# Turning the experts' gate and up results by threes instead of one wave at a time

## The chip, the cores and the metric

The kernel runs on one NeuronCore of a Trainium2 chip. The number that counts is the device time of one execution in microseconds (us); lower is better. TensorE (PE in the profile) multiplies, VectorE (DVE) and ScalarE (ACT) work element by element, GpSimd (POOL) does a few side jobs, and SyncE (SP) issues the DMA transfers. TensorE writes its results to PSUM, which has eight banks of 512 float32 numbers in each of 128 partitions; the other engines copy them from there to SBUF.

## The reference

Two layers of a decoder over 264 tokens (256 of a prompt, 8 of samples). The change lies in the last sub-layer of the second one, a mixture of eight experts of which each token uses two:

```python
def moe_swiglu(h, w_router, w_gate, w_up, w_down):
    logits = jnp.einsum('bld,de->ble', h, w_router).astype(jnp.float32)
    top_val, top_idx = lax.top_k(logits, TOP_K)          # TOP_K = 2
    gate = jax.nn.softmax(top_val, axis=-1)
    ...
    for e in range(N_EXPERTS):                           # 8
        act = jax.nn.silu(h @ w_gate[e]) * (h @ w_up[e])  # 1024 -> 1408 columns, twice
        out = out + combine[..., e:e + 1] * (act @ w_down[e])
    return out
```

Everything is float32. The token mixers, the cross-attention and the dense feed-forward of layer 0 fill the first three quarters of the time and are the same in both kernels.

## The kernel before

**Places, slots and waves.** The router's choices put each token into two of 768 places (`PLACES`). 32 places are a slot, which belongs to one expert: 8 slots are fixed, one for each expert, and 16 are free and go to experts that have more tokens than a slot holds. Four slots are a wave, so there are six waves (`WAVES`), of 128 places each.

**Pieces.** The experts' weights come in 66 pieces of 2 MB, each with a 128-row block of all eight experts' weights, 512 columns of each. 44 of them (`GU_PIECES`) are for gate and up: a column group `c_` has 256 gate and 256 up columns (`GU_COLS` = 256), and needs eight pieces, one for each 128 rows of the 1024; there are five such groups (`GU_FULL` = 5) and a last one with 128 columns of each, in four pieces. 22 pieces are for the down product. They lie in a ring of four places in the tile `big`; SP issues piece p when piece p-4 is no longer read (line 492). Since a free slot's expert is only known at run time, VectorE (11 of 16) and ScalarE (5 of 16) first copy the cells of the free slots to fixed addresses in `stream` and `nrm` (`copies`, lines 2273 and 1666), wave by wave, for waves 2 to 5 of the next piece.

**A wave on TensorE** (`wave`, line 1180) is four matmuls, one for each slot, of 32 places by 512 columns. Each uses 32 columns of the array, so the four run side by side; each is two instructions in the profile, so a wave has eight. Its results are added up over the pieces of a group in bank w of PSUM, for wave w.

**The end of a group.** After the group's last piece, ScalarE takes silu of the gate half of bank w (`silu`, line 1674), VectorE multiplies it with the up half (`multiply`, line 2282) into the tile `m_a[w]` (a part of `tmp`). The result has places on partitions, and the down product needs it with columns on partitions. So TensorE turns it (`turn`, line 1165): two transposes of 128 x 128, which use the full array (one in the last group). They go to bank 6 or 7 in turn, and ScalarE (line 1682, even waves) or VectorE (line 2290, odd waves) copies them to `acts`, in `turned_in`.

**The order** is written out by hand on each engine. TensorE does the turns of a group during the first piece after it: the wave w of that piece, which overwrites bank w, then the turn w. That is in pieces 8, 16, 24, 32, 40 and 44. A turn waits for the multiplication of its wave (`m_act`) and for the eviction of the turn two before it (`m_even`, `m_odd`), since this had the same bank. VectorE and ScalarE take each instruction in its written order: in such a piece they go through w = 0 to 5, copy for the next piece where w is 2 or more, and evict the turn of the same w.

Of the kernel before, what the change touches and what calls it, by code (L numbers as in the profile page):

```python
# [24 lines left out]
P = 128  # L25
# [49 lines left out]
WAVES = (FIXED + FREE) // 4  # L75
PLACES = (FIXED + FREE) * SLOT
GU_COLS, GU_FULL = CELL // 2, F_TILES * P // (CELL // 2)
# [9 lines left out]
def gu_piece(p):  # L87

    return (p // KT, (p % KT,)) if p < GU_FULL * KT else (GU_FULL, (2 * (p - GU_FULL * KT), 2 * (p - GU_FULL * KT) + 1))


def gu_ends(p):

    return 0 <= p < GU_PIECES and KT - 1 in gu_piece(p)[1]
# [43 lines left out]
def program(nc, t):  # L138

    with ExitStack() as ctx:  # L140
# [116 lines left out]
        m_silu, m_act, m_turn = sem("m_silu"), sem("m_act"), sem("m_turn")  # L257
        m_even, m_odd = sem("m_even"), sem("m_odd")
# [9 lines left out]
        def bank(b, lo=0, n=512, rows=P, r0=0):  # L268
            return ps[r0:r0 + rows, b * 512 + lo:b * 512 + lo + n]
# [50 lines left out]
        ident, ones = c(C_ID), c(C_ONES)  # L320
# [111 lines left out]
        m_sig, m_a = ([tmp[:, GU_COLS * k:GU_COLS * (k + 1)] for k in range(a, z)] for a, z in ((0, 2), (2, 2 + WAVES)))  # L432
# [6 lines left out]

        def turned(n, cols):  # L440

            return bank(6 + n % 2, 0, cols)

        lin_of, piece_of, n, q = {}, {}, 0, 0
        for name, k, pieces in (("in", N_PROJ, 1), ("out", KT, 2), ("memk", KT, 1), ("q", KT, 1), ("memv", KT, 1), ("o", KT, 1)):
            lin_of[name], piece_of[name] = n, q
            n, q = n + k, q + k * pieces
# [126 lines left out]
        def _(pe):  # L574
# [62 lines left out]
            for l in range(DEPTH):  # L637
# [414 lines left out]
                for mt in range(2):  # L1052
                    ins = pe.transpose(bank(7, mt * P, P), csP[:, mt * P:(mt + 1) * P], ident)
# [14 lines left out]
                for dt in range(2):  # L1068
                    ins = pe.transpose(bank(7, dt * P, P), csO[:, dt * P:(dt + 1) * P], ident)
# [40 lines left out]
                for k in range(KT):  # L1110
                    pe.wait_ge(h_full, (3 * l + 2) * KT + k + 1)
                    ins = pe.matmul(bank(7, 0, NT, NE), wrt[:, k * NE:(k + 1) * NE], tile(tmp, k), start=k == 0, stop=k == KT - 1)
# [42 lines left out]
                                            start=tt == 0, stop=tt == 2, skip_group_check=True)  # L1155
                    ins.then_inc(gx, 1)

                def turn(c_, w):

                    n, cols = WAVES * c_ + w, GU_COLS if c_ < GU_FULL else P  # L1160
                    pe.wait_ge(m_act, n + 1)
                    if n >= 2:
                        pe.wait_ge((m_even, m_odd)[w % 2], n // 2)
                    for f in range(cols // P):
                        ins = pe.transpose(turned(n, cols)[:, f * P:(f + 1) * P], m_a[w][:, f * P:(f + 1) * P], ident)  # L1165
                    ins.then_inc(m_turn, 1)

                def wave(p, w, dst, rows, first, last, parts=1):

# [23 lines left out]
                for p in range(GU_PIECES):  # L1193
                    c_, ks = gu_piece(p)
                    if p < KT - 1:
                        gather(p + 1)
                    elif p == KT - 1:
                        slot_sums()
                    if p < KT:
                        pe.wait_ge(gx_act, p + 1)  # L1200
                        pe.wait_ge(gx_dve, p + 1)
                    for w in range(WAVES):
                        if ks[0] == 0 and c_:
                            pe.wait_ge(m_act, WAVES * (c_ - 1) + w + 1)
                        wave(p, w, w, lambda part: xg(ks[part]), ks[0] == 0, ks[-1] == KT - 1, len(ks))
                        if ks[0] == 0 and c_:
                            if (c_, w) == (1, 0):
                                pe.wait_ge(slots_in, 1)
                            turn(c_ - 1, w)
                for h in range(2):  # L1210
                    for f in range(F_TILES):
                        p = GU_PIECES + h * F_TILES + f
                        for w in range(WAVES):
                            if (h, f) == (0, 0):
                                pe.wait_ge(m_act, WAVES * GU_FULL + w + 1)
                            if h == 0 and w == 0 and f * P % GU_COLS == 0:
                                pe.wait_ge(m_even, (f * P // GU_COLS + 1) * WAVES // 2)
                                pe.wait_ge(m_odd, (f * P // GU_COLS + 1) * WAVES // 2)
                            elif (h, f) == (1, 0):
                                pe.wait_ge(out_lo, w + 1)  # L1220
                            wave(p, w, w, lambda part: acts(f), f == 0, f == F_TILES - 1)
                            if (h, f) == (0, 0):
                                turn(GU_FULL, w)
                        if h == 1 and 1 <= f <= 4:
                            if f == 1:
                                pe.wait_ge(out_lo, WAVES)
                                pe.wait_ge(picks, BACK)
                            elif f >= 3:
                                pe.wait_ge(m_add, f - 2)
                            scatter(0, f - 1, 6 + (f - 1) % 2)  # L1230
                        elif h == 1 and f == 7:
                            pe.wait_ge(m_add, KT // 2)
                            for j in range(KT // 2):
                                norm_part((l + 1) * NORMS, j, tmp)
# [12 lines left out]
        def _(act):  # L1247
# [35 lines left out]
            for l in range(DEPTH):  # L1283
# [222 lines left out]
                for j in range(KT):  # L1506
                    n = L0 + lin_of["memk"] + j
# [5 lines left out]
                for j in range(KT):  # L1513
                    n = L0 + lin_of["q"] + j
# [161 lines left out]
                def turned_in(c_, w):  # L1676

                    n, cols = WAVES * c_ + w, GU_COLS if c_ < GU_FULL else P
                    act.wait_ge(m_turn, n + 1)
                    f0 = c_ * (GU_COLS // P)  # L1680
                    dst = proj[:, ACTS + f0 * PLACES:ACTS + (f0 + cols // P) * PLACES].rearrange("p (f s) -> p f s", f=cols // P)[:, :, w * P:(w + 1) * P]
                    act.activation(dst, turned(n, cols).rearrange("p (f s) -> p f s", f=cols // P), ACT.Copy).then_inc(m_even, 1)
# [8 lines left out]
                for p in range(-1, PIECES_X):  # L1691
                    if 0 <= p < KT - 1:
                        gather_in(p + 1)
                    for w in range(WAVES):
                        if gu_ends(p):
                            act.wait_ge(wave_done, WAVES * p + w + 1)
                            silu(gu_piece(p)[0], w)
                        elif p - GU_PIECES in (F_TILES - 1, DOWN_PIECES - 1):
                            act.wait_ge(wave_done, WAVES * p + w + 1)
                            out_high((p - GU_PIECES) // F_TILES, w)  # L1700
                        if w >= 2 and p + 1 < PIECES_X:
                            copies(p + 1, w)
                        if w % 2 == 0 and p > 0 and gu_ends(p - 1):
                            turned_in(gu_piece(p - 1)[0], w)
                    if p == GU_PIECES + F_TILES + 5:
                        act.preload_act_table_set("natural_log_exp_and_others")
                        for j in range(KT // 2):
                            act.wait_ge(m_add, j + 1)
                            square(j, xT, tmp)
# [7 lines left out]
        def _(dve):  # L1717
# [42 lines left out]
            for l in range(DEPTH):  # L1760
# [523 lines left out]
                def turned_in(c_, w):  # L2284

                    n, cols = WAVES * c_ + w, GU_COLS if c_ < GU_FULL else P
                    dve.wait_ge(m_turn, n + 1)
                    f0 = c_ * (GU_COLS // P)
                    dst = proj[:, ACTS + f0 * PLACES:ACTS + (f0 + cols // P) * PLACES].rearrange("p (f s) -> p f s", f=cols // P)[:, :, w * P:(w + 1) * P]
                    dve.tensor_copy(dst, turned(n, cols).rearrange("p (f s) -> p f s", f=cols // P)).then_inc(m_odd, 1)  # L2290
# [14 lines left out]
                for p in range(-1, PIECES_X):  # L2305
                    if 0 <= p < KT - 1:
                        gather_in(p + 1)
                    if p == 0:
                        weights_in()
                    elif p == KT - 1:  # L2310
                        slots_taken()
                    f = p - GU_PIECES - F_TILES
                    for w in range(WAVES):
                        if gu_ends(p):
                            multiply(gu_piece(p)[0], w)
                        elif p - GU_PIECES in (F_TILES - 1, DOWN_PIECES - 1):
                            out_low((p - GU_PIECES) // F_TILES, w)
                        if w >= 2 and p + 1 < PIECES_X:
                            copies(p + 1, w)
                        if w % 2 == 1 and p > 0 and gu_ends(p - 1):  # L2320
                            turned_in(gu_piece(p - 1)[0], w)
                    if 1 <= f <= 4:
                        add_scattered(0, f - 1, 6 + (f - 1) % 2)
                for d in range(4):
# [300 lines left out]
```

## Time and profile before

| | |
|---|---|
| median of 3 runs | 1625.02 us (1619.92 to 1628.04) |
| the profiled execution | 1625.43 us, of which 1623.6 us from first to last instruction |
| granted TensorE clock, mean | 0.98 |
| TensorE busy | 1515.6 us, 93% |
| VectorE, ScalarE busy | 1020.5 us (63%), 827.0 us (51%) |
| DMA, mean | 225 GB/s |

Times in the rows are us from the first instruction. A row of the timeline names an engine, a line of the kernel, an operation, the tiles written and read, and how many instructions are merged. The start of a TensorE row is where its first matmul starts to stream; the duration shown goes to the last one's modelled end, and overlaps with the next row. So distances between starts are what to read.

### The profile page before, as it was taken

The numbers are of one execution on the slowest core, as the hardware profiler recorded it, in microseconds if no ns is written. First come the engines' busy times: TensorE is split into PE (matmuls) and PEld (weight loads), VectorE is DVE, ScalarE is ACT, GpSimd is POOL, SyncE is SP. The second block draws the span as 40 slices with busy tenths as digits, with TensorE's granted clock in tenths as the row PEclk, the third lists the DMA queues.
The fourth block names the chain that finished last, engine by engine and source line by source line (L and its number), as shares of the span: only waits on it lengthen the run. The fifth ranks groups of instructions, "written<-read, shape, count | busy, mean of one in ns | idle before, by whom it ended". The sixth has DMA issues, their size and how long they took to land.

```text
span 1623.6 us, 31559 instructions
## 1 busy us (share of the span) xinstructions
PE 1515.6 (93%) x12739; PEld 1178.2 (73%) x12739; DVE 1020.5 (63%) x2060; ACT 827.0 (51%) x1597; POOL 308.2 (19%) x301
## 2 busy tenths in 40 slices
PE   6999987899999999999999878999879999999998
PEld 5999965799878999989999667998754322234333
DVE  4855589555245565668555886552356777777765
ACT  4445547545344454544455465453424566665654
POOL 3992224200000000039912232000000100000000
PEclk9999999999999999999999999999989999999999
DMA  8455445554774464454554355547746899999982
GB/s 322 156 182 169 147 143 178 178 206 158 295 300 149 154 203 173 157 202 156 182 172 145 143 166 188 205 159 282 306 175 215 311 378 390 384 382 360 402 341 82
DMA packets 52069, 365.14 MB, mean 225 GB/s; under 512 B 5973, under 2 KB 10645, under 8 KB 22997
## 3 DMA queue, kind: packets, MB, share of 16 engines
q1 hardware_dynamic: 49732, 355.97, 59.6%
q0 software_dynamic: 2192, 7.15, 1.3%
q8 instruction: 102, 1.67, 0.4%
q14 instruction: 43, 0.34, 0.1%
HBM read 338.62 MB, written 24.48 MB: 224 GB/s over the span
## 4 chain that ended last, share of the span: by engine, by line
PE 84%; DVE 9%; ACT 3%; DMA 2%; issue 2%; SPq 0%; DVEq 0%; ACTq 0%
PE ps L1180 21%; PE ps L606 17%; PE ps L607 16%; PE ps L608 16%; DVE stream L1964 3%; PE ps L586 2%; DVE proj L2025 1%; PE ps L1145 1%; DMA ring<-w_o_dram 1%; PE ps L1165 1%; PE ps L997 1%; PE ps L971 1%; PE ps L1188 1%; DMA ring<-w_v_dram 1%; PE ps L873 1%
## 5 line engine op out<-in xcount | busy, mean ns | idle before, releaser
L317 DVE TENSOR_TENSOR wL<-ring,wH 128x1024 fp32r<-128x1024 f32 x284 | 357.6, 1263 | 322.6 <-ACT wH L311 320.6
L606 PE MATMUL ps<-hH,wH 128*128 128x264 f32 x1376 | 401.7, 292 | 14.6 <-DVE hL L1736 7.8
L607 PE MATMUL ps<-hL,wH 128*128 128x264 f32 x1376 | 393.6, 286 | 0.0
L608 PE MATMUL ps<-hH,wL 128*128 128x264 f32 x1376 | 393.2, 286 | 0.0
L311 ACT ACTIVATE wH<-ring 128x1024 fp32r<-128x1024 f32 x284 | 298.0, 1054 | 120.1 <-PE ps L608 109.6
L606 PEld LDWEIGHTS ps<-hH,wH 128*128 128x128 f32 x1376 | 262.3, 191 | 22.9 <-issue 19.7
L607 PEld LDWEIGHTS ps<-hL,wH 128*128 128x128 f32 x1376 | 263.0, 191 | 0.6
L608 PEld LDWEIGHTS ps<-hH,wL 128*128 128x128 f32 x1376 | 261.8, 190 | 0.0
L606 PE MATMUL ps<-projR,wH 128*128 128x264 f32 (+1 forms) x816 | 239.6, 294 | 15.7 <-DVE projR L2126 7.1
L607 PE MATMUL ps<-projR,wH 128*128 128x264 f32 (+1 forms) x816 | 233.7, 286 | 0.0
L608 PE MATMUL ps<-projR,wL 128*128 128x264 f32 (+1 forms) x816 | 233.1, 286 | 0.0
L1281 ACT ACTIVATE proj<-ps 128x264 f32<-128x264 f32 (+1 forms) x160 | 62.5, 390 | 277.4 <-PE ps L608 277.4
L2273 DVE COPY stream<-big 128x512 f32 x396 | 140.9, 424 | 86.9 <-PE ps L1180 86.8
L606 PEld LDWEIGHTS ps<-projR,wH 128*128 128x128 f32 x816 | 156.6, 192 | 19.9 <-DVE projR L2126 7.6
L607 PEld LDWEIGHTS ps<-projR,wH 128*128 128x128 f32 x816 | 156.7, 192 | 0.8
L608 PEld LDWEIGHTS ps<-projR,wL 128*128 128x128 f32 x816 | 156.3, 192 | 0.0
L1666 ACT ACTIVATE stream<-big 128x512 f32 x132 | 83.1, 631 | 113.8 <-PE ps L1180 113.8
L1666 ACT ACTIVATE nrm<-big 128x512 f32 x198 | 117.5, 626 | 30.7 <-PE ps L1180 30.7
L1180 PE MATMUL ps<-nrm,proj 128*32 128x512 f32 (+1 forms) x1120 | 127.1, 569 | 0.3 <-issue 0.3
L1180 PE MATMUL ps<-big,proj 128*32 128x512 f32 (+1 forms) x1120 | 127.1, 570 | 0.0
L1180 PE MATMUL ps<-stream,proj 128*32 128x512 f32 (+1 forms) x1120 | 126.8, 569 | 0.0
L2273 DVE COPY nrm<-big 128x512 f32 x330 | 117.8, 422 | 1.4 <-PE ps L1180 1.4
(372 smaller groups left out, 1907.8 us busy)
## 6 DMA issues: line engine op xcount, KB each, us to landing
big<-x_gu_dram SPq DMA_DIRECT2D x44, 2048.0 KB, 9.6
ring<-w_in_dram SPq DMA_DIRECT2D x56, 1024.0 KB, 4.8
big<-x_down_dram SPq DMA_DIRECT2D x22, 2048.0 KB, 9.8
ring<-w_gu_dram SPq DMA_DIRECT2D x22, 1024.0 KB, 4.8
stream<-states_dram SPq DMA_DIRECT2D x32, 512.0 KB, 4.1
ring<-w_out_dram SPq DMA_DIRECT2D x16, 1024.0 KB, 4.9
o_states_dram<-stream SPq DMA_DIRECT2D x32, 512.0 KB, 3.2
ring<-kc_dram SPq DMA_DIRECT2D x16, 1024.0 KB, 6.5
```

The costliest lines, as they stand in the source:

```text
L311: act.activation(wH[:, buf * PIECE:buf * PIECE + n], slot(s, half * n, n), ACT.Copy).then_inc(hi_ready, 1)
L317: dve.tensor_tensor(wL[:, buf * PIECE:buf * PIECE + n], slot(s, half * n, n), f32(wH[:, buf * PIECE:buf * PIECE + n]), ALU.subtract).then_ ...
L586: ins = pe.matmul(bank(6, 0, w), ones, tile(src, s0 + j, 0, w), start=j == 0, stop=j == KT - 1, skip_group_check=True)
L606: pe.matmul(dst, wh, high(k0 + k), start=k0 + k == 0, stop=False)
L607: pe.matmul(dst, wh, low(k0 + k), start=False, stop=False)
L608: ins = pe.matmul(dst, wl, high(k0 + k), start=False, stop=k0 + k == k_all - 1)
L873: ins = pe.matmul(bank(7, 0, NT), ones, nrm[:, post_tile(p) + j * NT:post_tile(p) + (j + 1) * NT], start=j == 0, stop=j == tiles - 1)
L1180: ins = pe.matmul(ps[32 * q:32 * q + 32, dst * 512:dst * 512 + n], rows(part)[:, b * SLOT:(b + 1) * SLOT], src, start=first and part == 0, ...
L1281: act.activation(dst, src, func, scale=scale).then_inc(lin_free[n % 2], 1)
L1666: ins = act.activation(copy_of(j), big[:, bass.ds(source[j] + BIG_ORDER[p % 4] * BIG, CELL)], ACT.Copy)
L1964: ins = dve.scalar_tensor_tensor(out=S[:, at * P:(at + 1) * P], in0=bank(hf, b * P, P), scalar=k[:, at:at + 1], in1=S[:, at * P:(at + 1) * ...
L2273: ins = dve.tensor_copy(copy_of(j), big[:, bass.ds(source[j] + BIG_ORDER[p % 4] * BIG, CELL)])
```

## The change

Turns are now made by threes. After wave 2 of the piece come the turns of waves 0, 1 and 2, and after wave 5 those of waves 3, 4 and 5. Three turns need three places in PSUM, and six of them are cycled through banks 6 and 7: `turned` puts turns 0 to 5 in banks 6, 7, 6, 7, 6, 7, at columns 0, 0, 256, 256, 0, 0, so two turns share a bank. No engine may read a bank while a turn is written to its other half: all evictions therefore wait for the last turn of their three (`turned_with`), and the second three waits for all evictions of the first. VectorE and ScalarE evict at w = 2 and w = 5 of their loops, behind the copies for that w: ScalarE turns 0 and 2, VectorE turn 1, and then ScalarE turn 4, VectorE turns 3 and 5.

```diff
         def turned(n, cols):
-            return bank(6 + n % 2, 0, cols)
+            return bank(6 + n % 2, n % WAVES // 2 % 2 * GU_COLS, cols)
+
+        def turned_with(n):
+            return n // 3 * 3 + 3
...
-                def turn(c_, w):
-                    n, cols = WAVES * c_ + w, GU_COLS if c_ < GU_FULL else P
-                    pe.wait_ge(m_act, n + 1)
-                    if n >= 2:
-                        pe.wait_ge((m_even, m_odd)[w % 2], n // 2)
-                    for f in range(cols // P):
-                        ins = pe.transpose(turned(n, cols)[:, f * P:(f + 1) * P], m_a[w][:, f * P:(f + 1) * P], ident)
-                    ins.then_inc(m_turn, 1)
+                def turn_three(c_, w0):
+                    cols, before = GU_COLS if c_ < GU_FULL else P, WAVES // 2 * c_
+                    if w0:
+                        pe.wait_ge(m_even, before + 2)
+                        pe.wait_ge(m_odd, before + 1)
+                    elif c_:
+                        pe.wait_ge(m_even, before)
+                        pe.wait_ge(m_odd, before)
+                    for w in range(w0, w0 + 3):
+                        n = WAVES * c_ + w
+                        pe.wait_ge(m_act, n + 1)
+                        for f in range(cols // P):
+                            ins = pe.transpose(turned(n, cols)[:, f * P:(f + 1) * P], m_a[w][:, f * P:(f + 1) * P], ident)
+                        ins.then_inc(m_turn, 1)
...
                         if ks[0] == 0 and c_:
-                            if (c_, w) == (1, 0):
+                            if (c_, w) == (1, 2):
                                 pe.wait_ge(slots_in, 1)
-                            turn(c_ - 1, w)
+                            if w % 3 == 2:
+                                turn_three(c_ - 1, w - 2)
...
-                            if (h, f) == (0, 0):
-                                turn(GU_FULL, w)
+                            if (h, f) == (0, 0) and w % 3 == 2:
+                                turn_three(GU_FULL, w - 2)
...
-                    act.wait_ge(m_turn, n + 1)
+                    act.wait_ge(m_turn, turned_with(n))
...
-                        if w % 2 == 0 and p > 0 and gu_ends(p - 1):
-                            turned_in(gu_piece(p - 1)[0], w)
+                        if w % 3 == 2 and p > 0 and gu_ends(p - 1):
+                            for v in ((0, 2), (4,))[w // 3]:
+                                turned_in(gu_piece(p - 1)[0], v)
...
-                    dve.wait_ge(m_turn, n + 1)
+                    dve.wait_ge(m_turn, turned_with(n))
...
-                        if w % 2 == 1 and p > 0 and gu_ends(p - 1):
-                            turned_in(gu_piece(p - 1)[0], w)
+                        if w % 3 == 2 and p > 0 and gu_ends(p - 1):
+                            for v in ((1,), (3, 5))[w // 3]:
+                                turned_in(gu_piece(p - 1)[0], v)
```

TensorE's program in piece 16, from its wave 0 on, before (`ps<-const,tmp` 128x128 is a transpose, and the other rows are the four matmuls of a wave):

```order
L1180 MATMUL ps<-big,proj 32x512 [waits landed3,m_act]
L1180 MATMUL ps<-big,proj 32x512 x3
L1165 MATMUL ps<-const,tmp 128x128 [waits m_even,m_act]
L1165 MATMUL ps<-const,tmp 128x128
L1180 MATMUL ps<-big,proj 32x512 [waits landed3,m_act]
L1180 MATMUL ps<-big,proj 32x512 x3
L1165 MATMUL ps<-const,tmp 128x128 [waits m_odd,m_act]
L1165 MATMUL ps<-const,tmp 128x128
L1180 MATMUL ps<-stream,proj 32x512 [waits copied_act,copied_dve,m_act]
L1180 MATMUL ps<-stream,proj 32x512 x3
L1165 MATMUL ps<-const,tmp 128x128 [waits m_even,m_act]
L1165 MATMUL ps<-const,tmp 128x128
```

The same place in the changed kernel, where the wave is line 1190 and the transpose line 1175:

```order
L1190 MATMUL ps<-big,proj 32x512 [waits landed3,m_act]
L1190 MATMUL ps<-big,proj 32x512 x3
L1190 MATMUL ps<-big,proj 32x512 [waits landed3,m_act]
L1190 MATMUL ps<-big,proj 32x512 x3
L1190 MATMUL ps<-stream,proj 32x512 [waits copied_act,copied_dve,m_act]
L1190 MATMUL ps<-stream,proj 32x512 x3
L1175 MATMUL ps<-const,tmp 128x128 [waits m_act,m_odd,m_even]
L1175 MATMUL ps<-const,tmp 128x128
L1175 MATMUL ps<-const,tmp 128x128 [waits m_act]
L1175 MATMUL ps<-const,tmp 128x128
L1175 MATMUL ps<-const,tmp 128x128 [waits m_act]
L1175 MATMUL ps<-const,tmp 128x128
```

The three pairs of transposes have moved together behind the third wave, and the first of them carries the waits for evictions.

VectorE's program in piece 16, before, from the last copies for this piece's own wave 5 on (line 2273 is a copy of a free slot's cell, line 2290 an eviction of a turn):

```order
L2273 COPY nrm<-big 128x512 [waits wave_done]
L2273 COPY nrm<-big 128x512
L2290 COPY proj<-ps 128x2x128 [waits m_turn]
L2273 COPY stream<-big 128x512 [waits wave_done,landed2]
L2273 COPY stream<-big 128x512 x2
L2273 COPY stream<-big 128x512 [waits wave_done]
L2273 COPY stream<-big 128x512 x2
L2290 COPY proj<-ps 128x2x128 [waits m_turn]
```

The same place in the changed kernel (copies are line 2285, evictions line 2302):

```order
L2285 COPY nrm<-big 128x512 [waits wave_done]
L2285 COPY nrm<-big 128x512
L2285 COPY stream<-big 128x512 [waits wave_done,landed2]
L2285 COPY stream<-big 128x512 x2
L2302 COPY proj<-ps 128x2x128 [waits m_turn]
L2285 COPY stream<-big 128x512 [waits wave_done]
L2285 COPY stream<-big 128x512 x2
```

The eviction of turn 1 now stands behind the first three copies for the next piece; those of turns 3 and 5 stand together behind its last two.

## Rows read from the trace of the kernel before

**Rows 1.** The chain that ended last, from 1220 us on, by line.
```profile
by line: PE ps L1180 85.9%; PE ps L1145 4.2%; PE ps L1165 3.1%; PE ps L1188 2.9%; PE ps L586 1.0%; DVE tmp L1729 0.7%; PE ps L1154 0.5%; ACT proj L1656 0.1%; issue 0.1%; ACT rstd L1267 0.1%; DVE xT L2302 0.1%; ACT rstd L1268 0.1%; ACT tmp L
```

**Rows 2.** Busy time of each engine in two stretches, granted clock, DMA share.
```profile
core 0: us, PE busy (x) PEld busy (x) DVE busy (x) ACT busy (x) POOL busy (x), PEclk, DMA share, GB/s
1225.50:1613.60 388.10, 387.84 (x3609) 135.62 (x3608) 283.77 (x814) 227.41 (x406) 6.89 (x6) 1.00 0.87 337
1333.80:1370.80 37.00, 37.00 (x346) 11.03 (x345) 27.27 (x80) 23.14 (x42) 0.00 (x0) 1.00 0.97 383
```

**Rows 3.** The instructions of line 1165, the turns, in the whole run.
```profile
L1165 PEld LDWEIGHTS ps<-const,tmp x66: 137/140/143, 1282.3 to 1489.3; 128*128 128x128 f32 x66
```

**Rows 4.** Timeline of TensorE, piece 15 and, from 1325.58, piece 16.
```profile
1320.43 1.90 PE L1180 MATMUL ps<-big,proj 128*32 128x512 f32 x16
...
1325.58 1.04 PE L1180 MATMUL ps<-big,proj 128*32 128x512 f32 x8
1326.56 0.44 PE L1165 MATMUL ps<-const,tmp 128*128 128x128 f32 x2
1326.92 1.07 PE L1180 MATMUL ps<-big,proj 128*32 128x512 f32 x8
...
1333.38 0.44 PE L1165 MATMUL ps<-const,tmp 128*128 128x128 f32 x2
```

**Rows 5.** Timeline of TensorE in piece 44: first and last of six turns.
```profile
1483.02 0.33 PE L1165 MATMUL ps<-const,tmp 128*128 128x128 f32 x1
...
1489.30 0.33 PE L1165 MATMUL ps<-const,tmp 128*128 128x128 f32 x1
```

**Rows 6.** Timeline of TensorE in the attention of the same layer.
```profile
1155.43 0.66 PE L1023 MATMUL ps<-const,conv 128*128 128x128 f32 x4
1155.93 0.60 PE L1029 MATMUL ps<-const,proj 128*128 128x128 f32 x4
1156.46 1.07 PE L987 MATMUL ps<-ring,tmp 128*32 128x256 f32 x16
```

**Rows 7.** Timelines of TensorE's matmuls and loads: 16 transposes of the router.
```profile
1204.41 1.97 PE L1119 MATMUL ps<-const,tmp 128*128 128x128 f32 x16
```
```profile
1204.41 1.73 PEld L1119 LDWEIGHTS ps<-const,tmp 128*128 128x128 f32 x16
```

**Rows 8.** Timeline of VectorE in piece 16.
```profile
1327.69 0.42 DVE L2282 TENSOR_TENSOR tmp<-tmp,ps 128x256 f32<-128x256 f32 x1
1328.02 0.76 DVE L2273 COPY nrm<-big 128x512 f32 x2
1328.69 0.42 DVE L2290 COPY proj<-ps 128x256 f32<-128x256 f32 x1
1329.49 1.10 DVE L2273 COPY stream<-big 128x512 f32 x3 [0.37 <-PE ps L1180]
```

**Rows 9.** Timeline of ScalarE in piece 16.
```profile
1329.48 0.63 ACT L1666 ACTIVATE stream<-big 128x512 f32 x1 [1.95 <-PE ps L1180]
1330.02 0.37 ACT L1682 ACTIVATE proj<-ps 128x256 f32<-128x256 f32 x1
```

**Rows 10.** Timelines of TensorE and VectorE in piece 8.
```profile
1281.35 1.04 PE L1180 MATMUL ps<-big,proj 128*32 128x512 f32 x8
```
```profile
1284.69 0.75 DVE L2273 COPY nrm<-big 128x512 f32 x2
```

**Rows 11.** DMA issues of pieces: all 54 from 1284 us on, then two alone.
```profile
DMA to landing us min/median/max: 7.9/9.9/11.0
```
```profile
L492 SPq DMA_DIRECT2D big<-x_gu_dram x1: 327/327/327, 1296.6 to 1296.6; - x1
...
DMA to landing us min/median/max: 10.4/10.4/10.4
```
```profile
L492 SPq DMA_DIRECT2D big<-x_gu_dram x1: 328/328/328, 1322.4 to 1322.4; - x1
...
DMA to landing us min/median/max: 9.5/9.5/9.5
```

## The prediction

> **What bounds the kernel now.** I read the chain of waits first, because it says which engine's faster work would move the end. From the first expert piece on it stays on TensorE: the waves have 85.9% of it and the turns (line 1165) 3.1% [rows 1]. Then the busy times over that whole stage, 1225.5 to 1613.6 us: TensorE is busy for 387.84 of 388.10 us at full granted clock (1.00, which is 2.4 GHz), VectorE for 283.77 and ScalarE for 227.41 [rows 2]. So here every microsecond taken from TensorE's stream is one off the end, unless something it waits for comes too late. One number warns: DMA is 97% busy where waves run without turns [rows 2]. I come back to it.
>
> **What a turn costs now.** Piece 15 has six waves and no turn: from 1320.43 to 1325.58 they take 0.858 us each [rows 4]. With a turn of two transposes behind each, the distance from turn to turn is (1333.38 - 1326.56) / 5 = 1.364 us [rows 4], so the turn costs 0.506. In piece 44, with one transpose, it is (1489.30 - 1483.02) / 5 = 1.256 us [rows 5], so 0.398. The difference of the two, 0.108 us, is one transpose. What is left, 0.506 - 2 x 0.108 = 0.290 us, is paid for each visit, however many transposes it has: TensorE goes from matmuls on 32 columns of the array, four side by side, to one on all 128, and back. It shows as both an entry and an exit: the turn's start is 0.98 us behind the wave's (0.12 more than 0.858), and the next wave starts 0.36 after the turn (0.15 more than two transposes) [rows 4].
>
> **What the change removes.** Six visits in each of pieces 8, 16, 24, 32, 40 and 44 are 36; now there are two in each, 12. The 66 transposes [rows 3] stay. So the sum is 24 visits x 0.290 = **7.0 us less**. It rests on two assumptions. First, that transposes in a row keep 0.108 us each. Sixteen of the router's take 1.97 us with the last one's drain of about 0.27, so (1.97 - 0.27) / 15 = 0.113, and their loads (1.73 - 0.14) / 15 = 0.106 [rows 7]; by the dearer one the 42 transposes that now follow another across a wave's or a pair's border cost at most 0.2 us more. Second, that a visit costs the same when it is longer. The trace has the very case: eight transposes between two runs of 32-column matmuls take 1156.46 - 1155.43 = 1.03 us, which is 8 x 0.108 + 0.16, one entry, although the second four belong to another line with waits of its own [rows 6]. So waits that are already satisfied, in the middle of such a run, cost nothing that I can see; I take zero, and as the dear end 0.07 us (half of a load's 0.14 [rows 3]) for each of the 24 middle waits, 1.7 us.
>
> Against this stands a rule that gives another price. It would be that a transpose cannot load while another streams, since both need all rows of the array. Then each costs its load and its stream, 0.140 [rows 3] + 0.107 (a wave streams 512 columns in two passes in 0.858 us, so 128 in one pass take 0.107) = 0.247, a pair 0.494 of the 0.506, and a visit only 0.012: the change would gain 24 x 0.012 = 0.3 us. The rows speak against it: a second transpose adds 0.108, not 0.247 [rows 4, 5], and the router's sixteen would take 3.9 us instead of 1.97 [rows 7]. By this rule the trace disagrees: the Trainium skill, page "TensorE: Matmul & The Clock Gate", section "The mechanism", says that a weight load overlaps with matmuls in flight only when its row group differs.
>
> **What the change moves, in piece 16.** TensorE first. Wave 0 starts at 1325.58 [rows 4]; three waves and the entry give 1325.58 + 2.57 + 0.12 = 1328.27 for the first three turns, six transposes and the exit 0.65 + 0.15, so wave 3 starts at 1329.07. Three more waves and an entry: the second three turns at 1331.76 us.
> - *Results needed earlier.* Wave 5 overwrites bank 5 and would start at 1330.8 instead of 1332.4. Its multiplication, the last, ends at 1328.11, and the copies for it at 1328.78 [rows 8]. Slack 2.0 us.
> - *Evictions.* The second three waits for turns 0 and 2 on ScalarE and turn 1 on VectorE. VectorE is free at 1328.78, takes the three copies for the next piece (wave 2 is done by then), 1.0 us net, and evicts in 0.42 [rows 8]: about 1330.2, 1.5 us before 1331.76. ScalarE has one copy of 0.63 and two evictions of 0.37 [rows 9], which wait for the three turns (done with drain at about 1329.2): 1330.0. Behind them on both engines wait the copies for wave 3 of the next piece, which wave 3 of this piece allows only from 1330.0 on and which are needed five microseconds later. The evictions of turns 3, 4 and 5 end at about 1333.7; nobody waits for them before the next group.
> - *Piece 8* is the tightest, since VectorE comes late out of the slot sums. Wave 0 starts at 1281.35 [rows 10], so the second three at 1287.53. VectorE is free at 1285.44 [rows 10]; copies and eviction end at about 1287.1 even at the slower copies of that place. Slack 0.4 us, once; I take no wait.
> - *DMA.* A piece is issued behind wave 1 of the piece four before, and needed by the copies three pieces and a wave later, 16 us at least; the slowest landing took 11.0 us [rows 11]. That leaves 5 us.
>
> So the sum is made against the profiled execution: 1625.43 - 7.0 = 1618.4 us. That run lies 0.4 us over the median of 1625.02, which would give 1618.0. I say **1618.2 us**, 0.43% less. The three runs of before spread over 8.1 us, which is as much as 0.5% of the time, and 0.5% is about what a measurement of this kernel can tell from no change.
>
> **The rivals.**
> 1. *Half of it.* Waits inside the threes cost their dear end (1.7 us), and in some pieces the second three waits for VectorE's eviction of turn 1, which is now in order behind three copies. It would take about 0.3 us on each of six second visits to lose another 1.8. For it: the order of VectorE, and the 0.4 us of piece 8. Against: 1.5 us of slack in the four middle ones. Time 1625.4 - 3.5 = 1621.9. Chance 0.10.
> 2. *No gain, because weights come no faster.* DMA is at 97% [rows 2], and a group's eight pieces now take 8 x 5.15 + 3.04 = 44.2 us; with the change 43.1. If 5.53 us for a piece were what the transfers can do, TensorE would wait for all that it saves: 1625.4. Against it: the six pieces issued from 1296.6 to 1322.4 us, 5.16 us apart, needed 10.4 us at first and 9.5 at the end [rows 11]. A queue that was overfed would show a rising time; so one piece takes no more than 5.16. Chance 0.05. The rule on loads above has the same result, 1625.1, with chance 0.02.
> 3. *Slower.* The evictions of the first three come so late that TensorE stands before the second three. There are six such places, so 7.0 / 6 = 1.2 us each eat the gain, and with the slack of 1.5 us that means evictions 2.7 us later than worked out above; to be 8.1 us slower it takes 2.5 us of standing, 4 us later. That could be if VectorE's copies for the next piece wait for a late landing, as these stand ahead of the eviction now: TensorE would wait for the weights of the next piece already in this one. A landing 4 us late beyond its 5 us slack has no row that speaks for it. Time, with 2.5 us each, 1633. Chance 0.03.
> 4. *More than worked out*, as when fewer switches also free a few tenths in the waves between: 1616. Chance 0.02.
>
> **How the numbers follow.** The forecast has 0.78. Its own range is 1614 to 1622, the sum's bounds (a gain of 5.1, with both dear ends, to 7.2 us, with the rounding of the starts) and some 3 us for medians of few runs. The range for 8 in 10 goes further on both sides for the runs' own spread and takes in rival 1: 1612 to 1624.5. The bound for faster by over 0.5% lies at 1616.9, only 1.3 us from the forecast, so about four in ten of its chance and rival 4 fall there: 0.32. Slower by over 0.5% is rival 3 and a bad draw: 0.04. The rest is 0.64.
>
> **What the profile after would show.** Line 1175 with 66 transposes in runs of six (three in piece 44), each run and its exit about 0.80 us from its start to that of the next wave. From wave 0 of piece 16 to wave 0 of piece 17 about 7.0 us instead of 8.2. TensorE's loads idle before line 1175 twelve times instead of 36. VectorE's and ScalarE's evictions each behind their three, and no wait of TensorE for `proj` over 0.1 us. Landings still 8 to 11 us. The forecast is wrong if transposes inside a run are further apart than 0.12 us, if line 1175 waits for `proj` (VectorE or ScalarE), or if waves wait for the ring's DMA.

## The result, and the profile after

| | before | changed |
|---|---|---|
| median | 1624.19 us (1616.90 to 1629.89, 16 runs) | 1616.35 us (1610.48 to 1621.95, 16 runs) |
| profiled execution, span | 1623.6 us | 1618.7 us |

The ratio is 0.9954, with a 95% interval from 0.9938 to 0.9970: 7.5 us less, with 4.9 to 10.1 in the interval. The sum said 7.0. The kernel before was run again beside the experiments: its median was 1623.72 us beside experiments 1 to 3 and 5 (18 runs, of which two in a slower state are left out of the ratios) and 1627.42 us beside experiment 6 (11 runs). One execution can't show the gain well, since executions of one kernel spread over 11 to 13 us. So I read only the part of the trace in which all turns lie: **the stretch** from TensorE's first wave of piece 8 to its first wave of piece 45. One trace of each kernel is kept, so how far the stretch itself spreads is not measured; but where nothing was changed its parts repeat, as piece 15 takes 5.15 us in both kernels (1320.43 to 1325.58 before, 1321.16 to 1326.31 changed). Before, it begins at 1281.35 [rows 10], and the first of these rows of TensorE's timeline ends it; the second is the first matmul of the closing norm:

```profile
1489.56 1.92 PE L1180 MATMUL ps<-big,proj 128*32 128x512 f32 x16
...
1590.17 2.05 PE L586 MATMUL ps<-tmp,const 128*128 128x264 f32 x8
```

That is 208.21 us. TensorE's timeline of the changed kernel, where the wave is line 1190 and the turn line 1175, shows the beginning of the stretch, piece 16, and the end of the stretch (columns as in [rows 4]); the last row is again the norm's:

```profile
1283.22 1.90 PE L1190 MATMUL ps<-big,proj 128*32 128x512 f32 x16
...
1326.31 1.90 PE L1190 MATMUL ps<-big,proj 128*32 128x512 f32 x16
1328.03 1.04 PE L1190 MATMUL ps<-stream,proj 128*32 128x512 f32 x8
1329.00 0.87 PE L1175 MATMUL ps<-const,tmp 128*128 128x128 f32 x6
1329.80 1.07 PE L1190 MATMUL ps<-stream,proj 128*32 128x512 f32 x8
...
1332.52 0.87 PE L1175 MATMUL ps<-const,tmp 128*128 128x128 f32 x6
1333.32 1.92 PE L1190 MATMUL ps<-big,proj 128*32 128x512 f32 x16
...
1484.52 1.92 PE L1190 MATMUL ps<-big,proj 128*32 128x512 f32 x16
...
1585.18 2.05 PE L590 MATMUL ps<-tmp,const 128*128 128x264 f32 x8
```

The stretch is 1484.52 - 1283.22 = 201.30 us: **6.91 less**. Piece 16 takes 1333.32 - 1326.31 = 7.01 us, a visit with its exit 0.80 and its entry 0.12. The two profiled executions differ by only 4.9 us because the changed one reached piece 8 1.87 us later: 1283.22 against 1281.35. That part holds no changed instruction.

The transposes of line 1175, and the idle time of the weight loads ahead of them (us in all, times). There are 12 such places now, and there were 36 before:

```profile
L1175 PE MATMUL ps<-const,tmp x66: 272/273/329, 1285.9 to 1484.3; 128*128 128x128 f32 x66
its engine sat idle before it (us, times) until:
  issue: 9.2, 12
```

And the evictions in piece 16, from the timelines of VectorE and ScalarE:

```profile
1329.42 1.09 DVE L2285 COPY stream<-big 128x512 f32 x3
1330.43 0.42 DVE L2302 COPY proj<-ps 128x256 f32<-128x256 f32 x1
```
```profile
1329.91 0.66 ACT L1693 ACTIVATE proj<-ps 128x256 f32<-128x256 f32 x2
```

The last of the three ends at 1330.85, 1.7 us before the second three start at 1332.52.

### The profile page after: what moved, and what is told of

It reads as the page before. It is cut to its first block, busy times and chain, and to the rows that moved or that the text cites. A ratio compares the mean times of both kernels' runs of the same rounds, so it can differ in the third digit from the quotient of the medians.

```text
span 1618.7 us, 31536 instructions
## 1 busy us (share of the span) xinstructions
PE 1509.5 (93%) x12739; PEld 1181.8 (73%) x12739; DVE 1021.6 (63%) x2060; ACT 826.9 (51%) x1597; POOL 310.7 (19%) x301
## 3 DMA queue, kind: packets, MB, share of 16 engines
q8 instruction: 102, 1.67, 0.4%
## 4 chain that ended last, share of the span: by engine, by line
PE 84%; DVE 10%; ACT 3%; issue 2%; DMA 1%; SPq 0%; DVEq 0%; ACTq 0%
PE ps L1190 21%; PE ps L610 17%; PE ps L611 16%; PE ps L612 16%; DVE stream L1976 3%; PE ps L590 2%; DVE proj L2037 1%; PE ps L1149 1%; PE ps L975 1%; PE ps L1001 1%; DMA ring<-w_o_dram 1%; PE ps L1198 1%; PE ps L1014 1%; DVE wL L317 1%; PE ps L877 1%
## 6 DMA issues: line engine op xcount, KB each, us to landing
big<-x_down_dram SPq DMA_DIRECT2D x22, 2048.0 KB, 10.1
```

## The experiments

All are read by the same stretch: 208.2 us before, 201.3 changed.

**1. Visits of two turns.** From the changed kernel, with pairs behind waves 1, 3 and 5, and a bank for each turn again:

```diff
-            return bank(6 + n % 2, n % WAVES // 2 % 2 * GU_COLS, cols)
+            return bank(6 + n % 2, 0, cols)
...
-                            if w % 3 == 2:
-                                turn_three(c_ - 1, w - 2)
+                            if w % 2:
+                                turn_three(c_ - 1, w - 1)
```

> Turns by twos: 18 visits of the full array instead of 36 before and 12 in the changed kernel, each turn with a bank of its own. Measured by the stretch from the first wave of piece 8 to the first wave of piece 45, which is 208.2 us before and 201.3 changed. Theory 'switch' (a visit costs 0.29 us however many transposes it has): 18 x 0.29 = 5.2 us less than before, a stretch of 203.0, a run of about 1619. Rival 'spacing' (the gain comes from the evictions or the waits no longer interleaving with every wave, so any grouping brings most of it): about 201.5, as with threes. Rival 'two banks' (the gain needs the shared banks): 208.

Median 1617.21 us (12 runs), ratio to before 0.9967 [0.9951, 0.9984]. Its timeline of TensorE:

```profile
1276.31 1.90 PE L1187 MATMUL ps<-big,proj 128*32 128x512 f32 x16
...
1280.82 0.63 PE L1172 MATMUL ps<-const,tmp 128*128 128x128 f32 x4 [0.17 <-issue]
...
1479.54 1.92 PE L1187 MATMUL ps<-big,proj 128*32 128x512 f32 x16
```

The stretch is 203.23 us, 4.98 less than before with 18 visits less; the 0.2 over the expected 203.0 are one short stand before a visit in piece 8 (the row with 0.17). The gain follows the number of visits, and shared banks are not needed for it. "Spacing" and "two banks" fall. They fall by the stretch alone: the runs, expected at 1619, can't tell pairs from threes, since this median lies only 0.9 us over that of the changed kernel.

**2. Half of each turn.** The kernel before with `for f in range(1)` in `turn`, which leaves out the second transpose of each turn.

> The kernel before with only the first of a turn's two transposes (the second is left out, so half of the experts' hidden values are not what they should be): 36 visits, 36 transposes instead of 66. It measures what a transpose costs inside a visit. Theory 'switch': 30 x 0.108 = 3.2 us less, a stretch of 205.0 us. Rival 'serial loads' (each transpose loads and streams in turn, 0.247 us, and a visit costs nearly nothing): 30 x 0.247 = 7.4 us less, a stretch of 200.8.

```profile
1285.19 1.04 PE L1180 MATMUL ps<-big,proj 128*32 128x512 f32 x8
1286.16 0.33 PE L1165 MATMUL ps<-const,tmp 128*128 128x128 f32 x1
1286.42 1.06 PE L1180 MATMUL ps<-big,proj 128*32 128x512 f32 x8
...
1490.14 1.92 PE L1180 MATMUL ps<-big,proj 128*32 128x512 f32 x16
```

Its one run took 1626.07 us, which lies among the runs of before (1616.90 to 1629.89) and says nothing of 3 us. In TensorE's timeline the stretch is 204.95 us, 3.26 less for 30 transposes: 0.109 us each. Serial loads, which asked for 200.8, are ruled out here. The rule of the page "TensorE: Matmul & The Clock Gate" of the Trainium skill, section "The mechanism", that a load overlaps with matmuls in flight only in other row groups, does not hold for these transposes; the measurement decides. The same section also lets a load into a background buffer go ahead of matmuls in flight; that would fit the 0.109 us, but no row here shows into which buffer a load goes.

**3. Turns without a change of the array's division.** The kernel before, with each transpose as four matmuls by the identity:

```diff
-                        ins = pe.transpose(turned(n, cols)[:, f * P:(f + 1) * P], m_a[w][:, f * P:(f + 1) * P], ident)
+                        for q in range(4):
+                            ins = pe.matmul(ps[32 * q:32 * q + 32, (6 + n % 2) * 512 + f * P:(6 + n % 2) * 512 + (f + 1) * P],
+                                            m_a[w][:, f * P + 32 * q:f * P + 32 * q + 32], ident, start=True, stop=True)
```

> The kernel before with each transpose made as four matmuls by the identity on 32 columns of the array each, side by side, like a wave's: 36 visits as before, but no change between 32 and 128 columns. Each takes two passes, so 128 columns of moving data cost 0.214 us instead of 0.108. Theory 'switch' (the 0.29 us is the change of the array's division): a turn of two costs 0.43 us instead of 0.506 and the single one 0.21 instead of 0.398, so 30 x 0.078 + 6 x 0.184 = 3.4 us less, a stretch of 204.8 us. Rival 'any visit' (the 0.29 us is paid by any foreign matmul between two waves, for its loads or semaphores): 30 x 0.214 + 6 x 0.107 = 7.1 us more, a stretch of 215.3.

```profile
1280.57 1.04 PE L1182 MATMUL ps<-big,proj 128*32 128x512 f32 x8
1281.43 0.62 PE L1166 MATMUL ps<-const,tmp 128*32 128x128 f32 x16
1281.87 1.04 PE L1182 MATMUL ps<-big,proj 128*32 128x512 f32 x8
...
1485.65 1.90 PE L1182 MATMUL ps<-big,proj 128*32 128x512 f32 x16
```

Read the distances of TensorE's timeline again: wave to turn 0.86, which is the wave alone, and turn to wave 0.44 for sixteen instructions. Entry and exit are gone, although there are as many visits, and eight times as many instructions in a turn. The stretch is 205.08 us (204.8 expected, 215.3 if any visit had cost it); the one run took 1621.57 us, among those of before.

This run alone leaves two rivals, since its four matmuls are also no transposes, and take two instructions each where a transpose takes one. Other full-array matmuls settle both. Experiment 6 takes away two visits of the scatter, ordinary multiplications, and gains 0.33 us for each. And the closing norm in the changed kernel, four ordinary matmuls of two instructions each, starts 1.83 us behind the start of the two waves ahead of it (1583.35 to 1585.18), 0.11 more than the 1.72 that they take. So the 0.29 us is the price of going from four matmuls of 32 columns to one of 128 and back.

The weight loads show more of it. These are rows of their timelines, before and in this experiment:

```profile
1326.55 0.20 PEld L1165 LDWEIGHTS ps<-const,tmp 128*128 128x128 f32 x2 [0.84 <-issue]
```
```profile
1281.00 0.13 PEld L1166 LDWEIGHTS ps<-const,tmp 128*32 128x32 f32 x4 [0.30 <-issue]
```

Before, the wave has streamed by 1325.58 + 0.86 = 1326.44; the turn's first load starts 0.11 us after that, at the same time as its transpose (1326.56), and the next wave's load starts with its matmul at 1326.92 too. Here the first loads of the turn start 0.43 us ahead of its matmuls, while the wave still streams. So at a change of division no load was begun ahead. The page "TensorEngine Tiling (Array Packing)" of the Trainium skill, section "Key Properties", says that a change of tiling mode drains the array; the trace agrees, and prices it at 0.29 us there and back.

**4. Later evictions.** The changed kernel with idle copies ahead of VectorE's eviction of turn 1 (`range(3)`, and in the second kernel `range(9)`):

```diff
+                            for _ in range(3 if w == 2 else 0):
+                                st(dve.tensor_copy(scratch(52, 384), scratch(52, 384)))
                             for v in ((1,), (3, 5))[w // 3]:
                                 turned_in(gu_piece(p - 1)[0], v)
```

> The changed kernel with three idle copies on VectorE ahead of its eviction of turn 1, about 1 us in each of the six pieces. It tests the slack of the second three: in the changed kernel the eviction ends 1.7 us before they start in piece 16 (1330.85 to 1332.52) and 0.8 us before in piece 8. Theory 'covered' (evictions cost nothing until they are later than that slack): only piece 8 waits, 0.2 to 0.3 us, a stretch of 201.6 us. Rival 'already late' (TensorE waits for evictions in a way that the profile puts down to nothing): 1 us in each of six pieces, a stretch of 207.

```profile
1276.18 1.90 PE L1190 MATMUL ps<-big,proj 128*32 128x512 f32 x16
...
1282.89 0.84 PE L1175 MATMUL ps<-const,tmp 128*128 128x128 f32 x6 [0.43 <-issue]
...
1477.95 1.92 PE L1190 MATMUL ps<-big,proj 128*32 128x512 f32 x16
```

With some 1.2 us of delay TensorE stands only in piece 8, and the stretch is 201.77 us, 0.47 more than changed. "Already late", which asked for 207, falls. The one run took 1613.90 us, within the spread of the changed kernel.

> The same with nine idle copies, about 3 us. Theory 'covered': TensorE waits for what exceeds the slack, about 1.3 us in each of four pieces, 1.5 in piece 44 and 2.2 in piece 8, 9 us in all, a stretch of 210 us, and the wait shows on line 1175 with VectorE's eviction as its releaser; this eats the whole gain. If VectorE catches up only late, the waves of the next piece wait for its copies too, and it is more. Rival 'the delay is taken up elsewhere' (bank sharing and order don't bind): 201.5.

Its timelines of VectorE in piece 16, and of TensorE in pieces 8 and 16 and at the end of the stretch:

```profile
1326.65 3.52 DVE L2334 COPY const<-const 128x384 f32<-128x384 f32 x9
1330.21 0.42 DVE L2302 COPY proj<-ps 128x256 f32<-128x256 f32 x1
```
```profile
1274.96 1.90 PE L1190 MATMUL ps<-big,proj 128*32 128x512 f32 x16
...
1284.03 1.08 PE L1175 MATMUL ps<-const,tmp 128*128 128x128 f32 x6 [2.80 <-issue]
1285.04 3.33 PE L1190 MATMUL ps<-big,proj 128*32 128x512 f32 x16
1288.19 1.89 PE L1190 MATMUL ps<-stream,proj 128*32 128x512 f32 x16
...
1325.20 0.88 PE L1175 MATMUL ps<-const,tmp 128*128 128x128 f32 x6
...
1330.73 0.84 PE L1175 MATMUL ps<-const,tmp 128*128 128x128 f32 x6 [1.94 <-issue]
...
1493.92 1.92 PE L1190 MATMUL ps<-big,proj 128*32 128x512 f32 x16
```

The stretch is 218.96 us, 17.7 more than changed, where I expected 9. Two things account for it. The nine copies took 3.56 us, not 3: in piece 16 the visits lie 5.53 us apart instead of 3.52, so TensorE stood 2.0 us, which is 3.56 less a slack of 1.55 (the eviction ends at 1330.63 and the turn starts 0.10 later; the 1.67 us between the two in the changed kernel less this 0.10 are the slack). The four pieces with turns after it did the same within 0.04. With 2.9 in piece 8 that is 12.8 us. The other 4.8 are the clock. These windows show the 6 us behind each of the six second visits; the column behind POOL's is the granted clock, 1.00 for 2.4 GHz:

```profile
1284.00:1290.00 6.00, 5.97 (x42) 2.07 (x46) 3.90 (x12) 1.02 (x2) 0.00 (x0) 0.72 0.50 161
1331.00:1337.00 6.00, 6.00 (x58) 2.05 (x60) 5.55 (x17) 2.35 (x5) 0.00 (x0) 1.00 0.72 240
1376.00:1382.00 6.00, 6.00 (x42) 1.92 (x44) 3.85 (x13) 1.05 (x3) 0.00 (x0) 0.72 0.59 186
1423.00:1429.00 6.00, 6.00 (x60) 1.94 (x62) 5.55 (x18) 2.54 (x5) 0.00 (x0) 1.00 0.79 276
1468.00:1474.00 6.00, 6.00 (x81) 3.26 (x82) 3.85 (x12) 1.24 (x3) 0.00 (x0) 0.72 0.60 199
1493.50:1499.50 6.00, 6.00 (x55) 1.97 (x59) 5.61 (x18) 2.33 (x5) 0.00 (x0) 1.00 0.71 246
```

In three of the six the clock fell to its lower level of 1.2 GHz for a part of the 6 us (in windows of 1 us it is 0.50 from 1285 to 1287, 1377 to 1380 and 1469 to 1472), and in the first of them two waves took 3.15 us (1285.04 to 1288.19) instead of 1.75. The whole run came to 1629.85 us, beside 1628.88 of one run before on the same chip. I had also expected the wait to be put down to VectorE's eviction; the trace says "issue", though the turn in piece 16 starts 0.10 us after that eviction ends. So "issue" ahead of a line can hide a wait, and only the distance between starts shows it.

**5. One visit.** All six turns behind wave 2, in five groups; turns 4 and 5 go to bank 5, which wave 5 must wait for, and the first group keeps its threes:

```diff
+            if c_ and w >= 4:
+                return bank(5, w % 2 * GU_COLS, cols)
...
+                            if c_ >= 2 and w == 5:
+                                pe.wait_ge(m_even, taken(c_ - 1)[0] + 2)
```

> All six turns behind wave 2 of the piece, in five of the six groups (turns 4 and 5 go to bank 5, which wave 5 of the piece overwrites last and which ScalarE evicts first; the first group keeps its threes, since its multiplications come late): 7 visits. Theory 'switch': 5 visits fewer than the changed kernel, 1.45 us less, a stretch of 199.9 us, and a run of about 1615, 0.5% below the kernel before. Rival 'late evictions': wave 5 of the piece has only 0.8 us of slack behind ScalarE's evictions of bank 5, and the visit comes only 0.1 us after the last multiplication; if these are later than worked out, TensorE waits there for about 0.3 us in each of five pieces and the stretch stays at 201.3 or more.

Median 1615.72 us (7 runs), ratio 0.9946 [0.9917, 0.9975]. The timeline of TensorE, with piece 16 in the middle, and VectorE's last multiplication ahead of it:

```profile
1280.70 1.90 PE L1208 MATMUL ps<-big,proj 128*32 128x512 f32 x16
...
1325.51 1.04 PE L1208 MATMUL ps<-stream,proj 128*32 128x512 f32 x8
1326.75 1.50 PE L1193 MATMUL ps<-const,tmp 128*128 128x128 f32 x12 [0.20 <-issue]
1328.18 1.06 PE L1208 MATMUL ps<-stream,proj 128*32 128x512 f32 x8
...
1481.02 1.90 PE L1208 MATMUL ps<-big,proj 128*32 128x512 f32 x16
```
```profile
1325.90 0.42 DVE L2314 TENSOR_TENSOR tmp<-tmp,ps 128x256 f32<-128x256 f32 x1
```

The stretch is 200.32 us: 0.98 of the expected 1.45. The rest is a wait, not for evictions but for the last multiplication, the other half of the rival's condition: the wave's start and the turn's lie 1.24 us apart instead of 0.97. The multiplication ends at 1326.32, the transposes start 0.43 later. In pieces 24, 32 and 40 the same distance is 1.06, 1.08 and 1.05 us, so all four waited, for 0.55 us together. A part of it came back: behind such a wait the visit of twelve with its exit takes 1.43 us (1326.75 to 1328.18), and 1.46 in experiment 6, where nothing waits.

**6. One visit in all six groups, and scatters in pairs.** From the last one, with the first group too, wave 5's multiplication ahead of the copies for wave 4, and four visits of the scatter (full-array matmuls of another kind) made two:

```diff
-                            multiply(gu_piece(p)[0], w)
+                            if w < 5:
+                                multiply(gu_piece(p)[0], w)
+                            if w == 4:
+                                multiply(gu_piece(p)[0], 5)
...
-                            scatter(0, f - 1, 6 + (f - 1) % 2)
+                            scatter(0, f - 2, 6)
+                            scatter(0, f - 1, 7)
```

> All six groups turned in one visit behind wave 2 (6 visits), with the multiplication of wave 5 moved on VectorE ahead of the copies for wave 4, since in the kernel with one visit in five groups TensorE still stood 0.08 to 0.27 us before the visit for it; and the four scatter visits of the second down half (12 full-array matmuls each) made two visits of 24. Theory 'switch': turns 6 visits fewer than the changed kernel, 1.75 us, a stretch from piece 8 to piece 45 of 199.6 us; and from piece 45 to the norm's first matmul, which is 100.7 us in the changed kernel, 2 x 0.29 = 0.6 us less if a visit of other full-array matmuls costs the same. The run about 1614, 0.6% below the kernel before. Rival 'bank 5': evictions of turns 4 and 5 come too late for wave 5, or the copies for wave 4, which now stand behind one more multiplication, do: the stretch stays above 200.3.

Median 1614.59 us (6 runs), ratio 0.9924 [0.9901, 0.9947]. Its timeline of TensorE:

```profile
1280.87 1.90 PE L1203 MATMUL ps<-big,proj 128*32 128x512 f32 x16
1282.59 1.04 PE L1203 MATMUL ps<-stream,proj 128*32 128x512 f32 x8
1283.56 1.53 PE L1188 MATMUL ps<-const,tmp 128*128 128x128 f32 x12
1285.02 1.06 PE L1203 MATMUL ps<-stream,proj 128*32 128x512 f32 x8
...
1480.47 1.90 PE L1203 MATMUL ps<-big,proj 128*32 128x512 f32 x16
...
1580.46 2.05 PE L605 MATMUL ps<-tmp,const 128*128 128x264 f32 x8
```

The stretch is 199.60 us, as expected, and the distance from wave to turn 0.97 again. From piece 45 to the norm it is 99.99 us, in the changed kernel 1585.18 - 1484.52 = 100.66: 0.67 less for two visits less, 0.33 each. This kernel is the fastest of all by its stretches: 8.6 us under the kernel before in the first, 0.6 in the second. That is 0.57% of the time; the measured 0.76% has it just inside its interval (0.53 to 0.99%).

## Why the prediction was right

- **What bounds.** TensorE's stream still decides: in the stretch it is busy for 201.30 of 201.30 us in the changed kernel (208.21 of 208.21 before), at a granted clock of 1.00, and what was taken from it, 6.9 us, came off the end within the interval of the runs (4.9 to 10.1).
- **The price of a visit, 0.290 us.** Four kernels measure it. Changed: 6.91 / 24 = 0.288. By twos: 4.98 with 0.2 of standing, so 5.18 / 18 = 0.288. Experiment 5: 0.98 with 0.55 of standing, of which 4 x 0.03 came back, so (0.98 + 0.43) / 5 = 0.28, the least sure of the four. Experiment 6: 8.61 / 30 = 0.287. Experiment 3, with the scatter and the norm, shows what it is paid for.
- **Transposes in a row, 0.108 us.** 0.109 in experiment 2. The dear ends (satisfied waits inside a run, 1.7 us; a slower pace, 0.2) did not come: a visit of six with its exit takes 0.80 us, six times 0.108 and 0.15. Two slips of the prediction change nothing: the transposes that newly follow another are 24 (66 less 12 firsts now, 66 less 36 before), not 42, so its 0.2 us bound was wider than needed; and the 0.16 us left over in the attention's run of eight [rows 6] is an exit, as it is measured to the next wave's start, not an entry.
- **Evictions.** They ended 1.7 us before they were needed in piece 16 (1.5 predicted), and experiment 4 gives the slack as 1.55 us, reached by delaying one engine. In piece 8 it is larger than the 0.4 us of the prediction: a delay of about 1.2 us made 0.5 of standing, so 0.7. The mechanism of rival 3 exists, then, and no cause for it was there. Its price was too low: 2 us of standing in five places and 2.9 in one cost 17.7 us, since the clock fell too: rival 3 counted a microsecond of standing as a microsecond.
- **DMA.** In the changed kernel the landings of the pieces issued from 1287 us on took 7.8 to 11.6 us (8 to 11 predicted). With one visit the stretch draws its 37 pieces in 199.6 us, 5.4 us for each, and TensorE does not wait; rival 2's limit of 5.53 does not exist.
- **The size.** 7.5 us by the ratio, 6.9 by the stretch, 7.0 predicted. The forecast of 1618.2 us was 1.85 over the median: 1.0 because it started from 1625.2, which is above the median of before over 16 runs, and 0.85 because the medians differ by 7.8, well inside what the interval leaves open. That the two medians come so close to the sum is partly luck, as the interval is 5 us wide; the stretch is what confirms it.

## What to carry to other kernels

Where matmuls on 32 columns of the array and on all 128 alternate, count the visits, not the instructions: each there and back cost 0.29 us here, whatever it held, so put full-array work together as far as PSUM has room, and let the evictions lie behind waves that run anyway. Read the price from two places with one and two instructions in a visit: their difference is the instruction, the rest the visit. Then check the latest producer as well as the evictions, since gathering work in one place asks for its last input sooner (0.55 us in experiment 5), and mind that a stand of 2 us can cost more than 2 us.

## What I had not expected of the hardware

- After TensorE had stood for 1.9 to 2.8 us in an otherwise full stream, the granted clock fell to 1.2 GHz in three places of six, at a cost of about 1.6 us each; after the other three stands of the same 1.9 us it stayed at 2.4 GHz. What tells them apart is open.
- A transpose by four 32-column matmuls in two passes, 0.22 us, is dearer than a full-array transpose in one pass, 0.108, but without the 0.29 of the visit: between waves it is the cheaper one (0.22 against 0.40, and 0.44 against 0.51 for two). From three in a row on it would be the dearer one: an estimate from these numbers, 3 x 0.22 = 0.66 against 0.29 + 3 x 0.108 = 0.61, that no run tests.
